# Expert loop of a two-block transformer kernel: activations 512 wide, bias products in four row groups, indices made ahead of the scatter, a new order over the chunks

## The chip, the cores and the metric

One core of one Trainium2 chip runs the whole program. The metric is the device time of one execution in microseconds; the time before is the median of 3 runs. The chip has a matrix engine (TensorE, PE in the profile, with PEld for its weight loads), a vector engine (DVE), a scalar engine (ACT), GpSimd (POOL) and SyncE (SP), which only issues transfers here. Each engine works off its own instructions in order; semaphores join them.

## The reference, cut to what matters

The program computes two blocks of a transformer over 512 tokens of width 1024. Only one part of the first block changes, the mixture of 32 experts of which each token takes 4:

```python
hg, hl = jnp.split(xblk @ w_gu[e] + b_gu[e], 2, axis=-1)
hg = jnp.minimum(hg, SWIGLU_LIMIT)
hl = jnp.clip(hl, -SWIGLU_LIMIT, SWIGLU_LIMIT)
glu = hg * jax.nn.sigmoid(hg * SWIGLU_ALPHA)
return ((hl + 1.0) * glu) @ w_down[e] + b_down[e]
```

`w_gu[e]` is 1024 x 2048, `w_down[e]` is 1024 x 1024, all float32. The rows are weighted by the gate and added into the tokens' rows of the output.

## The kernel before, in words

`experts` runs over 32 experts. An expert takes up to 128 tokens (slots) and 12 chunks of weights of 1 MB (128 x 2048 float32): chunks 0 to 7 are gate and value columns, 8 to 11 the down projection. Every float32 product is made from three products of a faster type: ACT copies a chunk from `raw` to its rounded part `wh` (`high_part`, line 2110), DVE subtracts to get the rest `wl` (`low_part`, line 2156), and PE multiplies for each of four k tiles `wh` with the high part of x, `wl` with it, and `wh` with the low part (lines 2080 to 2082): 12 matmuls of 512 columns a chunk. `raw` holds 6 chunks (SP reloads a place as soon as its `wl` is made, line 1994), `wh` and `wl` hold 4 (`PARTS`), so ACT may begin chunk m when PE has ended chunk m-4 (`used`).

The gate and value columns are cut in four groups g of 256+256 columns; a group takes two chunks (first and second half of k) and one bank of `pu`, two banks in turn. PE first puts the bias in with one product of 128 rows, of which only two rows of `brow` are not zero (line 2068). After chunks 3, 5, 7 and 9, ACT and DVE make `hb`, 256 wide, from group 0, 1, 2, 3 (`activate`), and PE turns it to `pt` by two transposes after chunks 3, 5, 7 and 8 (`turn`, line 2053); ACT and DVE split that to `hh` and `hl` (`turned_high`, line 2126, `turned_low`, line 2168) after chunks 5, 7, 9 and 10. Chunks 8 to 11 multiply these into `pd`.

Around this runs the traffic of tokens. DVE makes a selection matrix for the next expert (`select`, chunk 1), PE counts with it (`slots`, after chunk 2), DVE makes the indices (`index`, chunk 4, lines 2184 to 2188), POOL gathers the rows of x by them (line 2006), PE transposes these after chunks 8 and 9 (`turn_x`, line 2045, into `px`), ACT and DVE split them to `Xh` and `Xl` (lines 2130 and 2173) after chunks 10 and 11. The result goes back so: ACT multiplies `pd` with the gates to `y` (`weighted`, line 2116) at chunks 0 and 1 of the next expert, POOL adds the rows into memory by an indirect transfer (line 2018), waits for its landing (`scattered`), and counts up `returned`. `index` waits for `returned` (line 2184), since it overwrites `idx` and `gneg`, of which there are two places. The order on each engine is written out by hand; on POOL it is gather, bias, scatter, wait for the scatter's landing.

Of the kernel before, what the change touches and what calls it, by code (L numbers as in the profile page):

```python
# [6 lines left out]
F32 = mybir.dt.float32  # L7
I32 = mybir.dt.int32
# [1932 lines left out]
def experts(K, x, gate_rows, b_down, pos, gpart, w, bias, x_rows, y_rows, raw, loaded):  # L1941

    nc = K.nc
    with ExitStack() as ctx:
# [6 lines left out]
        brow = K.sb(ctx, "brow", [P, 2 * FE], F32R)  # L1951
# [3 lines left out]
        idx = K.sb(ctx, "idx", [P, 2], I32)  # L1955
        gneg = K.sb(ctx, "gneg", [P, 2])
        rl = K.sb(ctx, "rl", [P, 256])
        sg = K.sb(ctx, "sg", [P, 256])
        vc = K.sb(ctx, "vc", [P, 256])
        hb = K.sb(ctx, "hb", [P, 2, 256])  # L1960
# [4 lines left out]
        pu = K.ps(ctx, "pu", [P, 2, 512])  # L1965
        pd = K.ps(ctx, "pd", [P, 2, 512])
        px = K.ps(ctx, "px", [P, 2, 512])
        pt = K.ps(ctx, "pt", [P, 256])
        pslot = K.ps(ctx, "pslot", [P, 512])
        with stage(nc, "bias_in", "w_high", "w_low", "used", "relu", "sigmoid",  # L1970
                   "h_ready", "own", "turned", "t_high", "t_low", "sel_ready", "slots_ready", "idx_ready", "gathered",
                   "x_turned", "x_high", "x_low", "y_ready", "scattered", "trash_ready", "ones_ready", "spared", "issued", "returned", "down_made",
                   "down_added") as (block, *sems):
            (bias_in, w_high, w_low, used, relu, sigmoid, h_ready, own, turned, t_high, t_low, sel_ready, slots_ready,
             idx_ready, gathered, x_turned, x_high, x_low, y_ready, scattered, trash_ready, ones_ready, spared, issued, returned, down_made, down_added) = sems
# [23 lines left out]
            def _(pool):  # L1999
                def bias_of(e):  # L2000
                    pool.dma_start(brow[0:2, :].bitcast(F32), bias[bass.ds(e, 1), :, :].rearrange("a b n -> (a b) n")).then_inc(bias_in, 16)
# [7 lines left out]
                def expert(e, odd, first, last):  # L2009
                    if not last:  # L2010
# [3 lines left out]
                        pool.wait_ge(used, e * CHUNKS + 8)  # L2014
# [3 lines left out]
                    pool.indirect_dma_start(y_rows, bass.IndirectOffsetOnAxis(idx[:, odd:odd + 1], 0), y[:, odd, :], None,  # L2018
# [13 lines left out]
            def _(pe):  # L2032
# [1938 lines left out]
```

## Time and profile before

| | |
|---|---|
| median of 3 runs | 3823.16 us (3814.76 to 3829.57) |
| profiled execution | 3835.94 us, of it 3834.2 us span |
| PE, DVE, ACT busy over the span | 91%, 66%, 50% |
| expert loop | 632.5 to 1855 us of the span, 1222.5 us |
| PE, DVE, ACT busy in the loop | 1177.19, 1114.57, 941.03 us |
| granted TensorE clock, DMA share, rate in the loop | 1.00, 0.93, 338 GB/s |

A stretch of the busy table gives, for each engine, busy microseconds and instructions in brackets. Matmuls are pipelined: a matmul of 512 columns is shown as 0.39 us, yet the next starts about 0.23 us after it, so on PE starts are to be compared with starts. A bracket at a row's end is the idle time before it and the engine and line that ended it.

### The profile page before, as it was taken

The numbers are of one execution on the slowest core, as the hardware profiler recorded it, in microseconds if no ns is written. First come the engines' busy times: TensorE is split into PE (matmuls) and PEld (weight loads), VectorE is DVE, ScalarE is ACT, GpSimd is POOL, SyncE is SP. The second block draws the span as 40 slices with busy tenths as digits, with TensorE's granted clock in tenths as the row PEclk, the third lists the DMA queues.
The fourth block names the chain that finished last, engine by engine and source line by source line (L and its number), as shares of the span: only waits on it lengthen the run. The fifth ranks groups of instructions, "written<-read, shape, count | busy, mean of one in ns | idle before, by whom it ended". The sixth has DMA issues, their size and how long they took to land. (4 is left out here: it accounts for less than half of the span.)

```text
span 3834.2 us, 45928 instructions
## 1 busy us (share of the span) xinstructions
PE 3497.8 (91%) x16744; PEld 2766.1 (72%) x16744; DVE 2549.7 (66%) x3090; ACT 1934.5 (50%) x2320; POOL 216.6 (6%) x137
## 2 busy tenths in 40 slices
PE   9998776999999999999589898899998998799998
PEld 7875265777777777777458776678886876568886
DVE  6644545999999899999456757456625776646542
ACT  4213223777777777777345435444415435534422
POOL 0000000111111111111010000010001000000000
PEclk9987786999999999999899999899999999899999
DMA  4100025999999999999312111122322112023231
GB/s 145 45 23 23 0 109 206 342 348 343 345 341 346 345 352 346 345 351 346 118 47 77 50 61 55 46 86 95 104 83 72 56 50 82 17 62 108 96 105 61
DMA packets 113041, 597.08 MB, mean 156 GB/s; under 512 B 17554, under 2 KB 18850, under 8 KB 62562
## 3 DMA queue, kind: packets, MB, share of 16 engines
q1 hardware_dynamic: 102658, 577.78, 42.1%
q0 software_dynamic: 10240, 17.33, 1.8%
q8 instruction: 97, 1.59, 0.2%
q14 instruction: 46, 0.38, 0.0%
HBM read 585.01 MB, written 26.80 MB: 160 GB/s over the span
## 5 line engine op out<-in xcount | busy, mean ns | idle before, releaser
L2156 DVE TENSOR_TENSOR wl<-raw,wh 128x2048 fp32r<-128x2048 f32 x384 | 870.6, 2288 | 55.8 <-ACT wh L2110 55.6
L2110 ACT ACTIVATE wh<-raw 128x2048 fp32r<-128x2048 f32 x384 | 718.5, 1904 | 0.0
L2080 PE MATMUL pu<-wh,Xh 128*128 128x512 f32 x1024 | 405.7, 396 | 10.9 <-DVE wl L2156 10.9
L2082 PE MATMUL pu<-wh,Xl 128*128 128x512 f32 x1024 | 400.7, 391 | 0.0
L2081 PE MATMUL pu<-wl,Xh 128*128 128x512 f32 x1024 | 400.6, 391 | 0.0
L3815 ACT ACTIVATE w_high<-w_raw 128x1024 fp32r<-128x1024 f32 (+1 forms) x120 | 137.1, 1146 | 333.1 <-PE acc L3789 172.0
L3846 DVE TENSOR_TENSOR w_low<-w_raw,w_high 128x1024 fp32r<-128x1024 f32 (+1 forms) x120 | 159.6, 1331 | 195.0 <-PE ps L3747 103.5
L3771 PE MATMUL ps<-x_high,w_high 128*128 128x512 f32 x656 | 255.2, 389 | 0.0
L3772 PE MATMUL ps<-x_low,w_high 128*128 128x512 f32 x656 | 255.2, 389 | 0.0
L2080 PEld LDWEIGHTS pu<-wh,Xh 128*128 128x128 f32 x1024 | 193.0, 188 | 55.1 <-DVE wl L2156 17.5
L2730 PE MATMUL acc<-x_high,w_high 128*128 128x512 f32 x528 | 226.4, 429 | 0.0
L2082 PEld LDWEIGHTS pu<-wh,Xl 128*128 128x128 f32 x1024 | 192.6, 188 | 42.6
L2081 PEld LDWEIGHTS pu<-wl,Xh 128*128 128x128 f32 x1024 | 192.8, 188 | 40.3
L2731 PE MATMUL acc<-x_low,w_high 128*128 128x512 f32 x528 | 212.5, 402 | 0.0
L3332 DVE TENSOR_TENSOR w_low<-w_raw,w_high 128x1024 fp32r<-128x1024 f32 (+1 forms) x120 | 137.4, 1151 | 112.6 <-PE acc L2736 74.4
L2080 PE MATMUL pd<-wh,hh 128*128 128x512 f32 x512 | 210.8, 412 | 0.0
L2081 PE MATMUL pd<-wl,hh 128*128 128x512 f32 x512 | 202.3, 395 | 0.0
L2082 PE MATMUL pd<-wh,hl 128*128 128x512 f32 x512 | 201.4, 393 | 0.0
L3747 PE MATMUL ps<-x_high,w_low 128*128 128x512 f32 x704 | 173.2, 389 | 0.0
L3060 ACT ACTIVATE w_high<-w_raw 128x1024 fp32r<-128x1024 f32 (+1 forms) x120 | 119.2, 996 | 95.0 <-PE lev L2926 79.7
L3747 PEld LDWEIGHTS ps<-x_high,w_low 128*128 128x128 f32 x704 | 132.2, 188 | 27.5
L3784 PE MATMUL acc<-h_high,w_high 128*128 128x512 f32 x352 | 143.1, 407 | 1.5 <-DVE h_low L3880 1.5
(681 smaller groups left out, 7059.2 us busy)
## 6 DMA issues: line engine op xcount, KB each, us to landing
raw<-in_exp_w SPq DMA_DIRECT2D x384, 1024.0 KB, 7.1
w_raw<-in_w_in SPq DMA_DIRECT2D x100, 512.0 KB, 3.4
w_raw<-in_w_up SPq DMA_DIRECT2D x88, 512.0 KB, 3.7
w_raw<-in_w_down SPq DMA_DIRECT2D x32, 704.0 KB, 4.0
w_raw<-in_w_out SPq DMA_DIRECT2D x32, 384.0 KB, 3.1
w_raw<-in_w_mem_kv SPq DMA_DIRECT2D x16, 512.0 KB, 4.5
w_raw<-in_w_out SPq DMA_DIRECT2D x8, 512.0 KB, 4.2
w_raw<-in_ple_gate_w SPq DMA_DIRECT2D x8, 512.0 KB, 3.8
```

What stands on the lines that cost most here:

```text
L2080: nc.tensor.matmul(o, lh[:, k, :], wh[:, m % PARTS, c], start=(m >= 8 and kh == 0 and kk == 0), stop=False)
L2081: nc.tensor.matmul(o, lh[:, k, :], wl[:, m % PARTS, c], start=False, stop=False)
L2082: mm = nc.tensor.matmul(o, ll[:, k, :], wh[:, m % PARTS, c], start=False, stop=end)
L2110: nc.scalar.activation(wh[:, m % PARTS, :], raw[:, m % RAW, :], ACT.Copy).then_inc(w_high, 1)
L2156: nc.vector.tensor_tensor(wl[:, m % PARTS, :], raw[:, m % RAW, :], wh[:, m % PARTS, :], ALU.subtract).then_inc(w_low, 1)
L2730: nc.tensor.matmul(o, wh[:, n % 3, c], hi[:, k, :], start=(k == 0), stop=False)
L2731: nc.tensor.matmul(o, wh[:, n % 3, c], lo[:, k, :], start=False, stop=False)
L3747: mm = nc.tensor.matmul(o, wl[:, u % 2, c], high[:, k, :], start=False, stop=(k == DT - 1))
L3771: nc.tensor.matmul(o, wh(u)[:, c], high[:, k, :], start=(k == 0), stop=False)
L3772: nc.tensor.matmul(o, wh(u)[:, c], low[:, k, :], start=False, stop=False)
L3784: nc.tensor.matmul(o, wh(u)[:, c], hh[:, f * PART + k, :], start=(f == 0 and k == 0), stop=False)
L3846: nc.vector.tensor_tensor(wl[:, u % 2, 0:width(u)], raw[:, u % 3, 0:width(u)], wh(u), ALU.subtract).then_inc(low_ready, 1)
```

## The change

- `pu` has four banks, one for each of: gate columns 0 to 511, value columns 0 to 511, gate 512 to 1023, value 512 to 1023. Each takes two chunks. `px` has no banks of its own now: it is the first two banks of `pu`.
- All four bias products are made at the expert's start (`biases`), each from 32 partitions of its own (`brow[32g:32g+32]`), after waits for the bias and for both halves of x. `brow` is loaded by four small transfers in place of one.
- The activation works twice an expert, 512 wide, cut in `gate` (ACT), `gated` and `valued` (DVE); the turn of `hb` is four transposes, within chunk 5 (after its second k tile) and within chunk 9 (after its first). `turned_high` and `turned_low` are 512 wide, at chunk 8 and at chunk 0 of the next expert; there stands the splitting of x too. `weighted` moves from chunks 0 and 1 to 2 and 3.
- `index` no longer waits for `returned` and moves to chunk 5; the gates' sum and a copy of the index for the scatter (`back`) are made by `pay` at chunk 8, which waits for `returned`. `select` moves to chunk 2.
- POOL's bias transfers wait for chunk 1's end rather than for chunk 7's. The weights' layout in memory follows the new grouping; `rest_of_experts` reads it so.

The diff, cut:

```diff
-                    pool.dma_start(brow[0:2, :].bitcast(F32), bias[bass.ds(e, 1), :, :].rearrange("a b n -> (a b) n")).then_inc(bias_in, 16)
+                    for g in range(4):
+                        pool.dma_start(brow[32 * g:32 * g + 2, :].bitcast(F32),
+                                       bias[bass.ds(e, 1), :, g * 512:(g + 1) * 512].rearrange("a b n -> (a b) n")).then_inc(bias_in, 16)
...
-                        pool.wait_ge(used, e * CHUNKS + 8)
+                        pool.wait_ge(used, e * CHUNKS + 2)
...
                 def turn(e, c, first):
-                    pe.wait_ge(h_ready, e * 4 + (c + 1))
+                    pe.wait_ge(h_ready, e * 2 + (c + 1))
                     if not (first and c == 0):
-                        pe.wait_ge(t_low, e * 4 + c)
-                    for i in (0, 1):
-                        mm = nc.tensor.transpose(pt[:, i * P:(i + 1) * P], hb[:, c % 2, i * P:(i + 1) * P], K.c("ident"))
+                        pe.wait_ge(t_low, e * 2 + c)
+                    for i in range(4):
+                        mm = nc.tensor.transpose(pt[:, i * P:(i + 1) * P], hb[:, c, i * P:(i + 1) * P], K.c("ident"))
                     mm.then_inc(turned, 1)
 
+                def biases(e):
+                    pe.wait_ge(bias_in, e * 64 + 64)
+                    pe.wait_ge(x_low, e * 2 + 2)
+                    for g in range(4):
+                        nc.tensor.matmul(pu[:, g, :], ones[32 * g:32 * g + 32, :], brow[32 * g:32 * g + 32, :], start=True, stop=False)
+
                 def expert(e, odd, first, last):
+                    biases(e)
                     for m in range(CHUNKS):
                         kh, g = halves(m)
                         pe.wait_ge(w_low, e * CHUNKS + (m + 1))
                         if m < 8:
-                            o, lh, ll = pu[:, g % 2, :], Xh, Xl
-                            if kh == 0:
-                                if g == 0:
-                                    pe.wait_ge(bias_in, e * 16 + 16)
-                                    pe.wait_ge(x_low, e * 2 + 1)
-                                if not (first and g < 2):
-                                    pe.wait_ge(h_ready, e * 4 + (g - 1))
-                                nc.tensor.matmul(o, ones[:, :], brow[:, g * 512:(g + 1) * 512], start=True, stop=False)
-                            elif g == 0:
-                                pe.wait_ge(x_low, e * 2 + 2)
+                            o, lh, ll = pu[:, g, :], Xh, Xl
                         else:
                             o, lh, ll = pd[:, g, :], hh, hl
-                            pe.wait_ge(t_low, e * 4 + (4 if kh else 2))
+                            pe.wait_ge(t_low, e * 2 + (kh + 1))
                             if kh == 0 and not first:
                                 pe.wait_ge(y_ready, e * 2 + (g - 1))
                         for kk in range(4):
@@ -2080,16 +2081,19 @@
                             nc.tensor.matmul(o, lh[:, k, :], wh[:, m % PARTS, c], start=(m >= 8 and kh == 0 and kk == 0), stop=False)
                             nc.tensor.matmul(o, lh[:, k, :], wl[:, m % PARTS, c], start=False, stop=False)
                             mm = nc.tensor.matmul(o, ll[:, k, :], wh[:, m % PARTS, c], start=False, stop=end)
-                        mm.then_inc(used, 1)
-                        if m in (3, 5, 7, 8):
-                            turn(e, 3 if m == 8 else (m - 3) // 2, first)
+                            if kk == 3:
+                                mm.then_inc(used, 1)
+                            if (m, kk) == (5, 1):
+                                turn(e, 0, first)
+                            if (m, kk) == (9, 0):
+                                turn(e, 1, first)
                         if not last:
                             if m == 2:
                                 slots(e + 1)
                             if m in (8, 9):
                                 turn_x(e + 1, m - 8)
...
                     act.wait_ge(used, e * CHUNKS + (11 + d))
                     if d == 0:
                         act.wait_ge(returned, e + 1)
+                        act.wait_ge(paid, e * 2 + 2)
                     nc.scalar.activation(y[:, odd, d * 512:(d + 1) * 512], pd[:, d, :], ACT.Copy, scale=gneg[:, odd:odd + 1]).then_inc(y_ready, 1)
 
-                def activate(e, g):
-                    act.wait_ge(used, e * CHUNKS + (2 * g + 2))
-                    nc.scalar.activation(rl[:, :], pu[:, g % 2, 0:256], ACT.Relu, scale=-1.0, bias=top[:, 0:1]).then_inc(relu, 1)
-                    act.wait_ge(relu, e * 4 + (g + 1))
+                def gate(e, c):
+                    act.wait_ge(used, e * CHUNKS + (4 * c + 2))
+                    nc.scalar.activation(rl[:, :], pu[:, 2 * c, :], ACT.Relu, scale=-1.0, bias=top[:, 0:1]).then_inc(relu, 1)
+                    act.wait_ge(relu, e * 2 + (c + 1))
                     nc.scalar.activation(sg[:, :], rl[:, :], ACT.Sigmoid, scale=-SWIGLU_ALPHA, bias=top[:, 1:2]).then_inc(sigmoid, 1)
 
                 def turned_high(e, c):
-                    act.wait_ge(turned, e * 4 + (c + 1))
-                    nc.scalar.activation(hh[:, 2 * c:2 * c + 2, :], pt[:, :].rearrange("p (a b) -> p a b", a=2), ACT.Copy).then_inc(t_high, 1)
+                    act.wait_ge(turned, e * 2 + (c + 1))
+                    nc.scalar.activation(hh[:, 4 * c:4 * c + 4, :], pt[:, :].rearrange("p (a b) -> p a b", a=4), ACT.Copy).then_inc(t_high, 1)
 
                 def x_part(e, half):
                     act.wait_ge(x_turned, e * 2 + (half + 1))
@@ -2133,19 +2138,23 @@
                 def expert(e, odd, first, last):
                     for m in range(CHUNKS):
                         high_part(e, m, first)
-                        if not first and m < AHEAD:
-                            weighted(e - 1, 1 - odd, m)
-                        if m in (5, 7, 9, 10):
-                            turned_high(e, 3 if m == 10 else (m - 5) // 2)
-                        if m in (3, 5, 7, 9):
-                            activate(e, (m - 3) // 2)
-                        if not last and m >= 10:
-                            x_part(e + 1, m - 10)
+                        if not first:
+                            if m == 0:
+                                turned_high(e - 1, 1)
+                                x_part(e, 0)
+                                x_part(e, 1)
+                            if m in (2, 3):
+                                weighted(e - 1, 1 - odd, m - 2)
+                        if m in (5, 9):
+                            gate(e, (m - 5) // 4)
+                        if m == 8:
+                            turned_high(e, 0)
...
-                def activate(e, g):
-                    dve.wait_ge(relu, e * 4 + (g + 1))
-                    nc.vector.tensor_scalar(vc[:, :], pu[:, g % 2, 256:512], SWIGLU_LIMIT, -SWIGLU_LIMIT, ALU.min, ALU.max).then_inc(own, 1)
-                    dve.wait_ge(sigmoid, e * 4 + (g + 1))
+                def gated(e, c):
+                    dve.wait_ge(sigmoid, e * 2 + (c + 1))
                     nc.vector.scalar_tensor_tensor(sg[:, :], rl[:, :], SWIGLU_LIMIT, sg[:, :], ALU.subtract, ALU.mult).then_inc(own, 1)
-                    dve.wait_ge(own, e * 8 + (2 * g + 2))
-                    nc.vector.scalar_tensor_tensor(hb[:, g % 2, :], vc[:, :], 1.0, sg[:, :], ALU.add, ALU.mult).then_inc(h_ready, 1)
+
+                def valued(e, c):
+                    dve.wait_ge(used, e * CHUNKS + (4 * c + 4))
+                    nc.vector.tensor_scalar(vc[:, :], pu[:, 2 * c + 1, :], SWIGLU_LIMIT, -SWIGLU_LIMIT, ALU.min, ALU.max).then_inc(own, 1)
+                    dve.wait_ge(own, e * 4 + (2 * c + 2))
+                    nc.vector.scalar_tensor_tensor(hb[:, c, :], vc[:, :], 1.0, sg[:, :], ALU.add, ALU.mult).then_inc(h_ready, 1)
...
                 def index(e, odd):
                     dve.wait_ge(slots_ready, e + 1)
+                    nc.vector.tensor_scalar(spare[:, :], pslot[:, 3:4], trash[:, 1:2], trash[:, 0:1], ALU.mult, ALU.add).then_inc(spared, 1)
+                    dve.wait_ge(spared, e + 1)
+                    nc.vector.tensor_tensor(idx[:, odd:odd + 1], spare[:, :], pslot[:, 2:3], ALU.add).then_inc(idx_ready, 1)
+
+                def pay(e, odd):
+
                     dve.wait_ge(returned, e + 1)
-                    nc.vector.tensor_scalar(spare[:, :], pslot[:, 3:4], trash[:, 1:2], trash[:, 0:1], ALU.mult, ALU.add).then_inc(spared, 1)
-                    nc.vector.tensor_reduce(gneg[:, odd:odd + 1], pslot[:, 0:2], AX.X, ALU.add, negate=True).then_inc(spared, 1)
-                    dve.wait_ge(spared, e * 2 + 2)
-                    nc.vector.tensor_tensor(idx[:, odd:odd + 1], spare[:, :], pslot[:, 2:3], ALU.add).then_inc(idx_ready, 1)
+                    nc.vector.tensor_reduce(gneg[:, odd:odd + 1], pslot[:, 0:2], AX.X, ALU.add, negate=True).then_inc(paid, 1)
+                    dve.wait_ge(idx_ready, e + 1)
+                    nc.vector.tensor_copy(back[:, odd:odd + 1], idx[:, odd:odd + 1]).then_inc(paid, 1)
 
                 def expert(e, odd, first, last):
                     for m in range(CHUNKS):
+                        if m == 0 and not first:
+                            turned_low(e - 1, 1)
                         low_part(e, m)
+                        if m == 0 and not first:
+                            x_part(e, 0)
+                            x_part(e, 1)
                         if not last:
-                            if m == 1:
+                            if m == 2:
                                 select(e + 1, False)
-                            if m == 4:
+                            if m == 5:
                                 index(e + 1, 1 - odd)
-                        if m in (3, 5, 7, 9):
-                            activate(e, (m - 3) // 2)
-                        if m in (5, 7, 9, 10):
-                            turned_low(e, 3 if m == 10 else (m - 5) // 2)
-                        if not last and m >= 10:
-                            x_part(e + 1, m - 10)
+                            if m == 8:
+                                pay(e + 1, 1 - odd)
+                        if m in (5, 9):
+                            gated(e, (m - 5) // 4)
+                        if m in (6, 10):
+                            valued(e, (m - 6) // 4)
+                        if m == 8:
+                            turned_low(e, 0)
```

## Rows read from the trace of the kernel before

**Rows 1.** The page's section 5: the two instructions that split a weight chunk.
```profile
L2156 DVE TENSOR_TENSOR wl<-raw,wh 128x2048 fp32r<-128x2048 f32 x384 | 870.6, 2288 | 55.8 <-ACT wh L2110 55.6
...
L2110 ACT ACTIVATE wh<-raw 128x2048 fp32r<-128x2048 f32 x384 | 718.5, 1904 | 0.0
```

**Rows 2.** Busy by stretch (PE, PEld, DVE, ACT, POOL, clock, DMA share, GB/s): two experts, 29.
```profile
1424.28:1461.27 36.99, 36.44 (x170) 29.69 (x169) 34.83 (x35) 29.43 (x29) 4.65 (x3) 1.00 0.98 353
...
1689.71:1726.77 37.06, 36.44 (x170) 29.65 (x169) 34.97 (x35) 29.37 (x29) 4.77 (x3) 1.00 0.98 362
...
701.34:1803.04 1101.70, 1066.59 (x4873) 859.64 (x4873) 1011.07 (x987) 852.62 (x813) 136.76 (x88) 1.00 0.95 346
```

**Rows 3.** Timeline of PE (start, duration, line): turns, x transposes, bias products, chunk edges.
```profile
1008.41 0.39 PE L2082 MATMUL pd<-wh,hl 128*128 128x512 f32 x1
...
1009.42 0.41 PE L2053 MATMUL pt<-const,hb 128*128 128x128 f32 x2 [0.62 <-DVE hl L2168]
...
1012.90 0.60 PE L2045 MATMUL px<-const,rows 128*128 128x128 f32 x4
...
1013.26 0.48 PE L2080 MATMUL pd<-wh,hh 128*128 128x512 f32 x1
...
1013.58 0.40 PE L2081 MATMUL pd<-wl,hh 128*128 128x512 f32 x1
...
1016.14 0.40 PE L2080 MATMUL pd<-wh,hh 128*128 128x512 f32 x1
...
1018.94 0.40 PE L2068 MATMUL pu<-brow,ones 128*128 128x512 f32 x1
...
1019.17 0.40 PE L2080 MATMUL pu<-wh,Xh 128*128 128x512 f32 x1
...
1021.93 0.39 PE L2080 MATMUL pu<-wh,Xh 128*128 128x512 f32 x1
...
1030.83 0.38 PE L2053 MATMUL pt<-const,hb 128*128 128x128 f32 x2
...
1030.96 0.48 PE L2068 MATMUL pu<-brow,ones 128*128 128x512 f32 x1
...
1031.28 0.40 PE L2080 MATMUL pu<-wh,Xh 128*128 128x512 f32 x1
```

**Rows 4.** Timeline of DVE: the first of the index instructions in one expert.
```profile
1032.43 0.28 DVE L2185 TENSOR_SCALAR spare<-pslot,trash 128x1 f32<-128x1 f32 x1 [2.43 <-POOLq L2021]
```

**Rows 5.** Waits, 700 to 1700 us (total us, times, longest).
```profile
DVE spare L2185 <- POOLq L2021: 33.5, 22, 2.9
...
PE pt L2053 <- DVE hl L2168: 16.2, 27, 0.6
```

**Rows 6.** Timeline of ACT: the second product of the gate with y in one expert.
```profile
1019.13 0.69 ACT L2116 ACTIVATE y<-pd,gneg 128x512 f32<-128x512 f32 x1 [0.30 <-PE pd L2082]
```

**Rows 7.** Timeline of POOL, then landing times of lines 2018 (scatter) and 2006 (gather).
```profile
1020.72 1.93 POOL L2018 DMA_INDIRECT y_rows<-y,idx  x1 [13.73 <-ACT y L2116]
...
1033.83 2.29 POOL L2006 DMA_INDIRECT rows<-x_rows,idx  x1 [11.18 <-DVE idx L2188]
...
DMA to landing us min/median/max: 6.3/10.1/12.1
...
DMA to landing us min/median/max: 5.8/9.0/10.8
```

**Rows 8.** Stretch with six chunks loading alone; then line 1994's landing times.
```profile
604.00:606.00 2.00, 0.00 (x0) 0.00 (x0) 0.00 (x0) 0.00 (x0) 0.00 (x0) 0.50 1.03 434
...
DMA to landing us min/median/max: 4.7/7.1/9.7
```

**Rows 9.** By tile pu, pt and px: duration ns min/median/max, first and last start.
```profile
L2097 PEld LDWEIGHTS pu<-gate_rows,b_down x8: 283/327/333, 616.1 to 624.8; 32*128 32x128 f32 x8
...
L2168 DVE TENSOR_TENSOR hl<-pt,hh x128: 416/418/421, 654.9 to 1844.5; 128x256 fp32r<-128x256 f32 x128
...
L2173 DVE TENSOR_TENSOR Xl<-px,Xh x64: 679/683/692, 631.9 to 1811.5; 128x512 fp32r<-128x512 f32 x64
```

More of the change, by code:

```diff
@@ L1950, in experts @@
         sel = K.sb(ctx, "sel", [P, NT, SLOTS], F32R)
-        brow = K.sb(ctx, "brow", [P, 2 * FE], F32R)
+        brow = K.sb(ctx, "brow", [P, 512], F32R)
         ones = K.sb(ctx, "ones2", [P, P], F32R)
@@ L1955, in experts @@
         idx = K.sb(ctx, "idx", [P, 2], I32)
+        back = K.sb(ctx, "back", [P, 2], I32)
         gneg = K.sb(ctx, "gneg", [P, 2])
[L1957 to L1960, printed above, removed]
+        rl = K.sb(ctx, "rl", [P, 512])
+        sg = K.sb(ctx, "sg", [P, 512])
+        vc = K.sb(ctx, "vc", [P, 512])
+        hb = K.sb(ctx, "hb", [P, 2, 512])
         top = K.sb(ctx, "top7", [P, 2])
@@ L1964, in experts @@
         y = K.sb(ctx, "y", [P, 2, D])
[L1965 removed]
+        pu = K.ps(ctx, "pu", [P, 4, 512])
         pd = K.ps(ctx, "pd", [P, 2, 512])
[L1967 to L1968 removed]
+        pt = K.ps(ctx, "pt", [P, 512])
         pslot = K.ps(ctx, "pslot", [P, 512])
+        px = pu
         with stage(nc, "bias_in", "w_high", "w_low", "used", "relu", "sigmoid",
                    "h_ready", "own", "turned", "t_high", "t_low", "sel_ready", "slots_ready", "idx_ready", "gathered",
[L1972 to L1973 removed]
+                   "x_turned", "x_high", "x_low", "y_ready", "scattered", "trash_ready", "ones_ready", "spared", "issued", "returned", "paid",
+                   "down_made", "down_added") as (block, *sems):
             (bias_in, w_high, w_low, used, relu, sigmoid, h_ready, own, turned, t_high, t_low, sel_ready, slots_ready,
[L1975 removed]
+             idx_ready, gathered, x_turned, x_high, x_low, y_ready, scattered, trash_ready, ones_ready, spared, issued, returned, paid, down_made, down_added) = sems
             def halves(m):
@@ L2090, in expert @@
                                 turn_x(e + 1, m - 8)
-                down = [pu[:, 0, :], pu[:, 1, :], pd[:, 0, :], pd[:, 1, :]]
+                down = [pu[:, 2, :], pu[:, 3, :], pd[:, 0, :], pd[:, 1, :]]
                 slots(0)
@@ L2210, in _ @@
                 index(0, 0)
+                pay(0, 0)
                 nc.vector.memset(top[:, 0:1], SWIGLU_LIMIT).then_inc(ones_ready, 1)
@@ L2213, in _ @@
                 nc.vector.tensor_copy(ones[:, :], K.c("ones")).then_inc(ones_ready, 1)
-                for part in range(0, 2 * FE, P):
+                for part in range(0, 512, P):
                     ins = nc.vector.tensor_scalar(brow[:, part:part + P], K.c("ones"), 0.0, None, ALU.mult)
                 ins.then_inc(ones_ready, 1)
-                down = [pu[:, 0, :], pu[:, 1, :], pd[:, 0, :], pd[:, 1, :]]
+                down = [pu[:, 2, :], pu[:, 3, :], pd[:, 0, :], pd[:, 1, :]]
                 for i in range(DT):
@@ L2267, in _ @@
                             pe.wait_ge(glu, e * FJ + (j + 1))
-                            for bank, half in ((pg, 0), (pv, 256)):
-                                o = half + j % 2 * P
-                                b = j // 2 * 512 + o
+                            for bank, of in ((pg, 0), (pv, 1)):
+                                group, o = j // 4 * 2 + of, j % 4 * P
+                                b = group * 512 + o
                                 nc.tensor.matmul(bank[:, j % 2, :], brow[0:1, b:b + P], one_row[:, :], start=True, stop=False)
@@ L3904, in pack_experts @@
 def pack_experts(gu, down):
-    up = gu.reshape(EXPERTS, 2, 4, P, 2, 4, 256).transpose(0, 5, 1, 3, 2, 4, 6)
+    up = gu.reshape(EXPERTS, 2, 4, P, 2, 2, 512).transpose(0, 5, 4, 1, 3, 2, 6)
     dn = down.reshape(EXPERTS, 2, 4, P, 2, 512).transpose(0, 1, 4, 3, 2, 5)
@@ L3924, in lay_out @@
         "exp_w": pack_experts(i["exp_w_gu"][0], i["exp_w_down"][0]),
[L3926 removed]
+        "exp_b_gu": np.ascontiguousarray(i["exp_b_gu"][0].reshape(EXPERTS, 2, 2, 512).transpose(0, 2, 1, 3)).reshape(EXPERTS, 2 * FE),
         "exp_b_down": i["exp_b_down"][0],
```

13 lines of the change are left out of this document (7 added, 6 removed).

## The prediction

> **What bounds the kernel now.** I read the page's slices first: only the expert loop runs at a full clock with all engines and the DMA above nine tenths, and only the loop is changed. Then the busy table by expert: 29 experts take 1101.70 us, 37.99 each, while the fastest take 36.99 and 37.06 [rows 2]. Per expert PE is busy 1066.59/29 = 36.78 us, DVE 1011.07/29 = 34.86, ACT 852.62/29 = 29.40, so DVE has 3.1 us of air and PE almost none; PE is the engine to follow, and DVE feeds it. The granted clock is 1.00 there (2.4 GHz), so no gain lies in it.
>
> The waits then say what lies above 36.99. DVE waits 33.5 us in 1000 us for POOL's `returned` in front of `index`, up to 2.9 us at a time [rows 5]; in one expert it stood 2.43 us, until 11.71 us after the scatter had begun [rows 4, 7]. Behind it stood the next chunks' `wl`, and PE ran dry. Scatters land after 6.3 to 12.1 us [rows 7], which is why experts alternate between 37 and 39 us. The mean price is 37.99 - 36.99 = 1.00 us an expert. The fast experts keep one more stall: the last turn of `hb` and its wait for `hl`. The last matmul of chunk 8 starts at 1008.41, the next instruction could start 0.23 later, at 1008.64, and the transposes start at 1009.42 [rows 3]: 0.78 us, in each of 27 experts (the wait recurs with at most 0.6 us of modelled idle time [rows 5]). So PE's own work is 36.99 - 0.78 = 36.21 us an expert.
>
> **Part 1: index without the wait, `pay` late.** The wait goes to chunk 8 on DVE. Where is PE then? I count from the first bias product, T0. An up chunk is 1021.93 - 1019.17 = 2.76 at the head and about 2.73 on the mean of 12 matmuls at 0.2275 (my value, from 0.225 to 0.232 between starts), a down chunk 1018.94 - 1016.14 = 2.80 [rows 3]. DVE reaches `pay` after `wl` of chunk 8, which it can make once ACT has chunk 8 rounded, which needs PE's chunk 4 ended (T0 + 14.6); behind the activation that is about T0 + 19.2. The scatter begins 0.90 us after the second `y` is complete (1019.13 + 0.69 = 1019.82, scatter 1020.72 [rows 6, 7]). `weighted` now stands at chunks 2 and 3, where ACT gets to it at about T0 + 2.0 instead of T0 + 0.2, so the scatter begins at T0 + 3.6 instead of 1020.72 - 1018.94 = 1.8, and lands at the latest at T0 + 15.7. `pay` has 3.5 us of cover, so DVE's stall goes wholly: -1.00 us an expert. Its extra copy is a one-column instruction (0.15 to 0.28 us, [rows 4] for the longer one), on DVE's air. If the cover were gone, `pay` would cost PE nothing until PE had also used the 3 to 4 us that `wl` is ahead of it (below).
>
> What is late next: POOL. It still waits for the scatter's landing before the gather, in its own queue. Gather start = T0 + 3.6 + scatter + 0.9 (1033.83 - 1032.43, less 0.5 for the index instructions [rows 4, 7]); with the medians 10.1 and 9.0 [rows 7] the rows of x are there at T0 + 23.6. PE wants them after chunk 8: 0.45 (bias) + 8 x 2.73 + 0.45 (slots) + 0.45 (turn) + 2.80 = T0 + 26.0. Before, the same sum was 0.92 + 8 x 2.73 + 0.45 + 3 x 0.22 (turns, part 3) + 2.80 + 0.78 + 0.25 = T0 + 27.7, and up to 2.4 more where `index` stalled. Cover falls to 2.4 us; at the slowest of both, 12.1 + 10.8, it is late by 27.4 - 26.0 = 1.4. The spread of the two is about 1.3 us, so this happens now and then: I take 0.1 us an expert, with 0 and 1.4 as bounds. The four bias transfers come behind the gather on POOL and are covered by 12 us.
>
> **Part 2: bias products in row groups.** Before: four products, one in 1019.17 - 1018.94 = 0.23 us [rows 3], 0.92 us an expert. After: four of 32 rows one after another in the program. At best they run together: 0.23 us, gain 0.69. At worst they take turns as before: gain 0. Below nothing too: weights of 32 rows took 0.283 to 0.333 us to load [rows 9] at the half clock of that stage [rows 8], and I see no sign that few rows load sooner; four loads have to be made where one was, at 0.09 us or more each (a load and a transpose in 0.36/4 [rows 3]), and the load behind them needs the whole array. That could lose 0.2 us. I take 0.45 us for the block (four loads, then one product), a gain of 0.47. The Trainium skill (TensorE: Matmul & The Clock Gate, Part 3: Packing small matmuls) says that matmuls on four row groups ran 3.07 times as fast as one by one; 0.92/3.07 = 0.30 us would be its price, a gain of 0.62. No row here shows row groups.
>
> **Part 3: 512-wide activation.** PE: two transposes cost 0.13 + 0.32 - 0.23 = 0.22 us (1030.83, 1030.96, 1031.28), four cost 0.36 + 0.32 - 0.23 = 0.45 (1012.90, 1013.26, 1013.58) [rows 3]; four times 0.22 against twice 0.45 is even. DVE: 16 instructions of 0.418 us become 8 of 0.683 [rows 9]: 6.69 against 5.46, -1.2 us. ACT is likewise shorter. Nothing of that is on PE's path; DVE's air of 3.1 us becomes 2.0 in a shorter expert (35.8 - 34.86 + 1.23 - 0.15).
>
> **Part 4: the new order.** I walked one expert with a `wl` of 2.29 us (2.2 between starts) and a `wh` of 1.90 (1.8) [rows 1], each `wh` held back until PE has ended the chunk four earlier. `wl` is complete 3 to 4.5 us before PE wants it in every chunk. The first half's `hb` is complete at T0 + 14.9, its turn is due at 15.9. The second half's: DVE ends `wl` 10 at 25.3, then 1.35 us in `valued`, 26.65; the turn is due at 26.0 + 0.45 + 0.7 = 27.1, cover 0.45. Its low part is complete at 29.5, chunk 10 begins at 30.1, cover 0.6. x is split at T0 + 32.9, the bias products wait for it at 35.7. So the 0.78 us stall goes too: -0.78. The two thin covers are real: if either fails by 0.3 us it is paid once an expert.
>
> **Sum.** 36.21 - 0.47 + 0.1 = 35.84 us an expert, say 35.8, against 37.99: 2.2 us, by 30 experts 66, and 1 to 2 us for the first and last, which had no `returned` stall: 68. The fewer `brow` instructions at the start hide under PE's down products. Profiled execution 3835.9 - 68 = 3768. It stood 12.8 us above the median of 3823.2; from that, 3755.
>
> **The rivals.**
> A, the row groups take turns: 0.92 us, the rest as forecast; 36.3 an expert, 1.7 x 31 = 53, 3770. Nothing in the trace speaks against it.
> B, the DMA becomes the bound. It carries 353 GB/s x 36.99 us = 13.06 MB an expert, with a busy share of 0.98 [rows 2]; if busy means full, it ends at 360 GB/s and an expert at 36.3, and with bursts uneven 36.5: 1.5 x 31 = 46, 3777. Against it: with chunks alone the same engines moved 434 GB/s at 1.03 [rows 8], ACT never waited for a chunk (the idle time before `wh` is 0.0) [rows 1], and chunks landed in 4.7 to 9.7 us [rows 8] where the ring leaves 13. The Trainium skill (DMA: Bandwidth & Descriptors, Where 436 GB/s comes from) says that loads from HBM are bound at about 358 GB/s a core, by which an expert takes 13.06/358 = 36.5 us, rival B's time; the 434 GB/s of this trace, also from HBM, speaks against that rule here.
> C, the gather is late as a habit, by 1 us on the mean, because at a higher rate both indirect transfers land about 1.7 us later each: 36.8, 1.2 x 31 = 37, 3786.
> D, slower than before: the same chain, scatter's landing, POOL, gather, `turn_x`. It decides when scatter plus gather exceed 26.0 - 4.5 + 2.15 = 23.7 us on the mean, against 19.1 by medians and 22.9 by the two slowest. With the slowest of both and one chunk more (1 MB at 434 GB/s, 2.4 us) in front, 25.3, PE stands 3.8 us at `turn_x`: 39.5 an expert, +1.5 x 31 = 47, 3870.
>
> **How the numbers follow.** Forecast 0.52; A 0.15; B 0.13; C 0.10; D 0.05; something between C and D that ends near the old time 0.05. The forecast's own range is 3738 to 3770: the bias block from 0.23 to 0.7, the gather from 0 to 0.4, and 7 us for medians of a few runs. To hold 8 in 10 the range must reach over A, B and most of C: 3734 to 3796. About 0.5% (19 us) is what a measurement here can tell from no change. Faster by more: forecast, A, B and nearly all of C, 0.88; within: 0.07; slower: 0.05.
>
> **What would show each step.** After: no DVE wait at `index`, and none to speak of at `pay`; an expert every 35.8 us; in PE's timeline 0.3 to 0.5 us from the first bias product to the first weight product (0.9 if A); no wait of the transposes in chunk 9 for `hb`, or that margin was wrong; the x transposes waiting for the gather only in a few experts (C, D if in most); ACT waiting for a DMA if B. The prediction is wrong if PE's own work isn't 35.7 us, which its matmul starts would show, or if the landing times of the indirect transfers grow by over 2 us each.

## The result, and the profile after

The changed kernel takes 3763.97 us (median of 4 runs, 3754.99 to 3776.01) against 3825.81 for the kernel before on the same occasions: a ratio of 0.9837, 95% interval 0.9815 to 0.9858, 62 us faster. 3755 was forecast, with a range of 3734 to 3796. Later, in a comparison of its own, it took 3762.07 us, a ratio of 0.9826 (0.9808 to 0.9845).

Most of the gain lies in the expert loop. Between the two profiled executions the span fell by 59.8 us, where 68 was forecast: 52.3 of it from the loop's first bias product to its last down product, about 7 behind the loop. That last stretch took 1973.6 to 1982.9 us in the fourteen profiled executions of this document, longest in the kernel before, so most of those 7 us may be variation from run to run; whether the change has a share in them is open. The first two experts became 2.3 us slower together (76.75 to 79.03), where the forecast had a small gain; one part of that is a late gather, the rest was not traced.

The lines of the page after that answer to those of before (the splits of a chunk are those of [rows 1]):

```profile
span 3774.4 us, 45043 instructions
PE 3472.6 (92%) x16744; PEld 2751.5 (73%) x16744; DVE 2520.7 (67%) x2854; ACT 1906.4 (51%) x2128; POOL 271.2 (7%) x233
...
L2165 DVE TENSOR_TENSOR wl<-raw,wh 128x2048 fp32r<-128x2048 f32 x384 | 873.5, 2286 | 58.7 <-ACT wh L2114 58.5
L2114 ACT ACTIVATE wh<-raw 128x2048 fp32r<-128x2048 f32 x384 | 735.4, 1916 | 191.2 <-PE pu L2083 144.5
```

ACT now stands 191.2 us before its `wh`, because PE has not yet freed a place, where it stood 0.0 before: the feeding engines are ahead of PE nearly all the time. The busy table by expert, with the columns of [rows 2]; three experts, then 29 of them:

```profile
900.64:940.45 39.81, 37.63 (x169) 30.34 (x168) 34.32 (x28) 28.59 (x23) 7.62 (x6) 0.96 0.92 337
940.45:976.23 35.78, 35.78 (x169) 29.16 (x168) 33.99 (x28) 28.49 (x23) 5.51 (x6) 1.00 0.99 359
...
1515.24:1551.02 35.78, 35.78 (x169) 29.16 (x168) 33.93 (x28) 28.49 (x23) 6.11 (x6) 1.00 1.00 377
...
718.72:1766.61 1047.89, 1041.57 (x4873) 845.88 (x4872) 986.47 (x783) 826.79 (x638) 187.66 (x174) 1.00 0.98 363
```

An undisturbed expert takes 35.78 us, PE busy in all of it; the mean is 1047.89/29 = 36.13 us, against 37.99. The difference of 0.35 us is in a few experts, and the waits of that stretch (total us, times, longest) say where:

```profile
PEld pu L2048 <- DMA rows<-x_rows,idx: 11.4, 14, 2.7
PEld pu L2063 <- issue: 10.4, 29, 0.4
PE pu L2048 <- DMA rows<-x_rows,idx: 6.2, 4, 2.3
```

Line 2048 is the transpose of x: it waits for the gather. PE stands idle for it in 4 of the 29 experts, and in 14 its weight load comes later for it. There is no wait of DVE for `returned` any more and none of PE for `hb` or `hl`, where [rows 5] had 33.5 and 16.2 us. The landing times (min/median/max) of the scatter, then the gather, and both on POOL's timeline:

```profile
DMA to landing us min/median/max: 6.3/11.3/12.6
...
DMA to landing us min/median/max: 4.6/9.7/11.7
...
1012.01 2.40 POOL L2021 DMA_INDIRECT y_rows<-y,back  x1 [19.10 <-ACT y L2121]
1024.95 1.65 POOL L2009 DMA_INDIRECT rows<-x_rows,idx  x1 [10.54 <-issue]
```

The expert begins at 1008.46 here. The scatter starts 3.55 us into it, as walked (3.6), and the gather 16.5 us into it, where the walk with the medians of before had 14.6.

### The profile page after: what moved, and what is told of

Read it like the earlier page. It is cut to its first block and busy times, and to the rows that moved or that the text cites. A ratio compares the mean times of both kernels' runs of the same rounds, so it can differ in the third digit from the quotient of the medians.

```text
span 3774.4 us, 45043 instructions
## 1 busy us (share of the span) xinstructions
PE 3472.6 (92%) x16744; PEld 2751.5 (73%) x16744; DVE 2520.7 (67%) x2854; ACT 1906.4 (51%) x2128; POOL 271.2 (7%) x233
## 5 line engine op out<-in xcount | busy, mean ns | idle before, releaser
L2114 ACT ACTIVATE wh<-raw 128x2048 fp32r<-128x2048 f32 x384 | 735.4, 1916 | 191.2 <-PE pu L2083 144.5
```

Of the source, the lines that this page charges most:

```text
L2114: nc.scalar.activation(wh[:, m % PARTS, :], raw[:, m % RAW, :], ACT.Copy).then_inc(w_high, 1)
```

## The experiments

Two theories stood at the start. Mine: PE's own work bounds the loop, and the gain is the sum of stalls and instructions taken out of PE's line, with a rest lost to late gathers. The rival: something the change brings besides (512-wide instructions, fewer instructions on DVE and ACT, another rhythm of the loads) is what pays. The first four kernels take parts one at a time; the others test what is left. Totals of variants that differ by a few us have overlapping intervals; there the time from one expert's first bias product to the next one's, read from the traces, decides. In undisturbed experts of one kernel it repeats within 0.1 us or better.

**Indices without the wait, alone, in the kernel before.**

```diff
                 def index(e, odd):
                     dve.wait_ge(slots_ready, e + 1)
-                    dve.wait_ge(returned, e + 1)
...
+                            if m == 8:
+                                pay(e + 1, 1 - odd)
```

> The kernel before, with one part of the change: the indices are made without waiting for the scatter's return, and the gates' sum and a copy of the index for the scatter are made at chunk 8, behind that wait. My theory: the stall of DVE at the index goes, every expert takes the 37.0 us of the fast ones instead of 38.0, the gain is 1.0 x 30 = 30 us (3795 against 3825). Rival: the wait only moves, to POOL, which starts the gather after the scatter has landed, and PE then waits at the transposes of x: 38 us an expert, no gain. By the medians the rows of x are there at 1.8 + 10.1 + 0.9 + 9.0 = 21.8 us after the expert's first bias product, and PE wants them at 27, so I expect no such wait.

Measured: 3797.25 us against 3829.64, ratio 0.9912 (0.9896 to 0.9929), 32 us. Every expert after the first takes 36.95 to 37.00 us; the alternation is gone. What is left in its waits is the old stall at the last turn:

```profile
PEld pt L2054 <- DVE hb L2166: 31.7, 29, 1.1
PE pt L2054 <- DVE hl L2170: 20.1, 29, 0.7
```

The wait was worth 1.02 us an expert and did not move to POOL: there the scatter starts early in the expert and the gather has room.

**The last turn inside chunk 9, alone and with the first.**

```diff
-                        if m in (3, 5, 7, 8):
-                            turn(e, 3 if m == 8 else (m - 3) // 2, first)
...
+                            if (m, kk) == (9, 0):
+                                turn(e, 3, first)
```

> The kernel before, with one thing changed: the last turn of hb stands in chunk 9 behind its first k tile instead of after chunk 8. My theory: the 0.78 us stall that every expert of the kernel before has at that turn goes, 0.7 to 0.8 x 32 = 22 to 25 us (3801), and the stalls behind the index stay. Rival: the stall moves to chunk 10, which needs the low part of the same turn, ready no earlier than about 1.9 us after chunk 9's start and behind a wl on DVE; then the gain is 0.3 us an expert or less, under 10 us.

> The kernel before with both parts: index free of the scatter's return, last turn inside chunk 9. If the two stalls are separate, 1.0 + 0.78 us an expert, about 55 us, 3770, and all that the changed kernel has beyond that is its bias block (0.4 to 0.5 us an expert, 15 us) less its late gathers (0.35 us, 11 us). Rival: the stalls overlap, or DVE (34.9 us of work in an expert of 36.2) becomes the bound: 36.7 or more, 3785 or above.

Measured: alone 3813.83 us, ratio 0.9957 (0.994 to 0.9974), 16 us, between the theory's 22 to 25 and the rival's 10; both 3783.14, ratio 0.988 (0.9864 to 0.9897), 46 us, 36.46 us an expert. The two add up (32 + 16), but the turn is worth 0.51 us an expert (36.97 - 36.46), not 0.78. The stall itself went wholly (0.86 us in the kernel with the index alone, none here). The waits of the kernel with both show part of what was given back:

```profile
PEld pu L2069 <- issue: 11.6, 28, 0.5
PEld pd L2081 <- DVE wl L2161: 6.9, 29, 0.2
```

The last turn had shared one break in the weight products with the transposes of x; alone it needs a break of its own (a place where other instructions stand between weight products). With the distances between PE's starts added up by kind over 28 experts of each kernel, the price of 0.35 us is: 0.09 for the late start behind the new break, 0.12 in the weight products, where PE now meets `wl`, 0.10 behind the bias products, and 0.15 in front of the first of them, less 0.11 in the transposes. The 0.15 is a wait for something that the profile does not name ("issue"): the first bias product starts 0.33 and 0.44 us after the product before it, in turn from expert to expert. In the kernel with the index alone that distance is 0.23.

**Bias products one after another, with 128 rows, in the changed kernel.**

```diff
-                        nc.tensor.matmul(pu[:, g, :], ones[32 * g:32 * g + 32, :], brow[32 * g:32 * g + 32, :], start=True, stop=False)
+                        nc.tensor.matmul(pu[:, g, :], ones[:, :], brow[:, g * 512:(g + 1) * 512], start=True, stop=False)
```

> The changed kernel with its four bias products of 128 rows each, one after another, as the kernel before makes them, at the expert's start; brow is 2048 wide and loaded by one transfer again. My theory: the row groups work, the block grows from about 0.55 us to about 0.95, fastest experts 36.15 instead of 35.78, 10 to 15 us slower than the changed kernel (3776). Rival A: row groups bring nothing and the time is that of the changed kernel (35.8). Rival B: the four small transfers on POOL make the gather late, so with one transfer the late gathers go and the median is no worse.

Measured: 3772.65 us, ratio 0.9848 (0.9831 to 0.9864); the fastest experts take 35.98 us (36.15 was expected), 0.20 more than 35.78. The mean is 36.21, with late gathers as in the changed kernel (landings of 11.4 and 9.8 us), so the four small transfers are not their cause. PE's timeline, first the changed kernel, then this one:

```profile
1008.13 0.40 PE L2083 MATMUL pd<-wh,hl 128*128 128x512 f32 x1
1008.46 0.51 PE L2063 MATMUL pu<-brow,ones 32*128 32x512 f32 x4
1008.90 0.50 PE L2081 MATMUL pu<-wh,Xh 128*128 128x512 f32 x1
1009.24 0.40 PE L2082 MATMUL pu<-wl,Xh 128*128 128x512 f32 x1
```

```profile
1035.06 0.40 PE L2081 MATMUL pd<-wh,hl 128*128 128x512 f32 x1
1035.30 1.08 PE L2061 MATMUL pu<-brow,ones 128*128 128x512 f32 x4
```

In row groups the four products start within 0.01 us of each other and take 0.44 us to the next start, but the first starts 0.33 - 0.23 = 0.10 late and the product behind them costs 0.34 - 0.23 = 0.11 more: 0.65 us. With 128 rows the block runs on without a gap, 0.92. That makes 0.27, and the periods give 0.20: the weight products outside the block take 0.06 us more in the kernel with row groups (the first ones behind it start every 0.235 to 0.24 us). The weight loads of both kernels at the same place:

```profile
1008.46 0.19 PEld L2063 LDWEIGHTS pu<-brow,ones 32*128 32x128 f32 x4 [0.36 <-issue]
1008.90 0.19 PEld L2081 LDWEIGHTS pu<-wh,Xh 128*128 128x128 f32 x1 [0.25 <-issue]
```

```profile
1035.06 0.89 PEld L2061 LDWEIGHTS pu<-brow,ones 128*128 128x128 f32 x4
```

With 128 rows each load starts with the product before its own, 0.23 us ahead. At the change from 128 to 32 rows, and at the change back, it starts only with its own product (1008.46 and 1008.90).

**The same with 32 rows in one row group** (on the changed kernel with `y` earlier, below).

```diff
+                        nc.tensor.matmul(pu[:, g, :], ones[0:32, :], brow[0:32, g * 512:(g + 1) * 512], start=True, stop=False)
```

> The same kernel, with the four bias products of 32 rows all on the first 32 partitions (brow 2048 wide again, one transfer). With 128 rows each one after another the block took 0.92 us, in four row groups 0.44 with 0.2 around it, and the expert 0.20 less. If the gain is that of four groups at once, one group takes the 0.92 us again, 36.0 an expert. If it is that of fewer rows, 35.8 stays.

Measured: 3783.75 us in a single run; 36.45 us an expert, 0.67 more than in four groups, and 0.47 more than with 128 rows.

```profile
1039.03 1.21 PE L2061 MATMUL pu<-brow,ones 32*128 32x512 f32 x4
1040.17 0.51 PE L2079 MATMUL pu<-wh,Xh 128*128 128x512 f32 x1
```

Both readings that I had written were off: one group takes not 0.92 but 1.14 us, with the same late starts around it. Four groups do run together (1.14 becomes 0.44), but 32-row products among 128-row ones cost more than 128-row ones do. The dearer part is at the edges: the second, third and fourth start 0.24 us apart, as full ones nearly do, while from the first to the second it is 0.34, and from the last to the weight product 0.32. That fits the loads above, which are not hidden where the row count changes; why they are not is not shown.

**The gather ahead of the wait for the scatter; `y` a chunk earlier.** Two independent cures of late gathers.

```diff
                         gather(e + 1, 1 - odd)
+                    if not first:
+                        pool.wait_ge(scattered, e * 16)
+                        pool.sem_inc(returned, 1)
```

```diff
-                            if m in (2, 3):
-                                weighted(e - 1, 1 - odd, m - 2)
+                            if m in (1, 2):
+                                weighted(e - 1, 1 - odd, m - 1)
```

> The changed kernel, where POOL starts the next gather as soon as its indices are made, and waits for the last scatter's landing only behind it. My theory: the late x transposes (the mean expert of 36.13 us against 35.78 for the undisturbed) come from POOL's queue, which holds the gather back until the scatter has landed; now the gather starts at about 11.6 us of an expert instead of 15, lands 3 us earlier, no expert waits for it, all take 35.8, 0.35 x 31 = 11 us less than the changed kernel. Rival: gather and scatter in flight together slow each other, landing times of both grow by 3 us or more, and the transposes of x wait as before (no gain).

> The changed kernel with the gate products of y behind chunks 1 and 2 on ACT instead of 2 and 3. My theory: the scatter starts 1.8 us earlier, so does the gather, and of the waits of up to 2.3 us at the x transposes only a rest of under 0.05 us an expert stays: 35.8 us, about 10 us less than the changed kernel. Rival: ACT waits for the last chunk's end before the second product, high parts come later, and PE waits for wl: 36.2 or more.

Measured: 3756.13 us (ratio 0.9821, 0.9805 to 0.9837) and 3759.08 us (0.9824, 0.9807 to 0.984). In both all experts after the first take 35.7 to 35.8 us and no wait for the gather is left. POOL with the gather first:

```profile
1030.29 2.40 POOL L2025 DMA_INDIRECT y_rows<-y,back  x1 [20.68 <-ACT y L2126]
1038.52 2.84 POOL L2009 DMA_INDIRECT rows<-x_rows,idx  x1 [5.83 <-DVE idx L2202]
```

It starts 8.2 us after the scatter instead of 12.9. So the late gathers come from POOL's queue. The rival was half right: landing in company takes longer (gather 10.4 us at the median instead of 9.7), which eats 0.7 of the 4.7 us. With `y` earlier, the scatter lands after 10.1 us at the median and the gather after 8.9, at a rate of 367 GB/s, where the changed kernel had 11.3 and 9.7 at 363: the load's mean rate alone does not set them. Nor does the moment of the start alone: the kernels below that also have `y` earlier and the old order on POOL land the gather after 8.5 to 8.7, but the scatter after 10.7 to 11.6. What sets the scatter's time is open.

**The wait put back into the changed kernel.**

```diff
                 def index(e, odd):
                     dve.wait_ge(slots_ready, e + 1)
+                    dve.wait_ge(returned, e + 1)
```

> The changed kernel with the one wait put back: the index waits for the scatter's return again. Two readings of what the wait costs. If its cost is the 1.0 us an expert of the kernel before, 37.1 us an expert and about 3795. If my walk through the new order holds, DVE reaches the index 10.3 us into the expert and the scatter returns at 15.1, a stall of 4 to 5 us; the first half of hb is then ready at 19 to 20 while PE wants to turn it at 15.9, so PE stands 3 to 4 us in every expert: 39 to 40 us, 3860 to 3890, slower than the kernel before. If the lead of wl over PE (3 to 4 us) absorbed it: 36.2, 3765.

Measured: 3863.84 us, ratio 1.0107 (1.0084 to 1.0129): slower than the kernel before. An expert takes 39.35 us.

```profile
DVE spare L2196 <- POOLq L2024: 99.3, 29, 5.4
PEld pt L2056 <- DVE hb L2175: 88.3, 44, 4.8
PE pt L2056 <- DVE hb L2175: 68.3, 28, 4.4
```

DVE stands 99.3/29 = 3.4 us an expert, PE at the first turn up to 4.4. One wait that cost 1.0 us in the old order costs 39.35 - 36.13 = 3.2 in the new one: the two parts of the change need each other. Some 0.6 of the 3.2 is not the wait itself but the lower of TensorE's two clock levels, which follows many of these stalls (last section); the granted clock of the 29 experts is 0.98 on the mean.

**The 512 width by itself** (on the kernel with `y` earlier): each 512-wide instruction of the activation and of the split of `hb` is cut in two.

```diff
-                    nc.vector.tensor_scalar(vc[:, :], pu[:, 2 * c + 1, :], SWIGLU_LIMIT, -SWIGLU_LIMIT, ALU.min, ALU.max).then_inc(own, 1)
+                    for h in (slice(0, 256), slice(256, 512)):
+                        ins = nc.vector.tensor_scalar(vc[:, h], pu[:, 2 * c + 1, h], SWIGLU_LIMIT, -SWIGLU_LIMIT, ALU.min, ALU.max)
+                    ins.then_inc(own, 1)
```

> The kernel with the gate products of y behind chunks 1 and 2 (no late gathers, every expert 35.78 us), with each 512-wide instruction of the activation and of the split of the turned hb cut in two of 256, on ACT and DVE. The 512 width by itself. My theory: PE is the bound and DVE has 1.8 us of air an expert; DVE gets 8 x (2 x 0.418 - 0.683) = 1.2 us more, that leaves 0.6, and the one thin cover, hb before the second turn (0.3 to 0.4 us), shrinks by 0.15: an expert stays at 35.8 to 35.9, under 5 us in all. Rival: DVE at 35.2 of 35.8 us can't keep its lead any more, PE waits for hb or wl, 36.3 or more, 15 us.

Measured: 3766.68 us, ratio 0.9832 (0.9815 to 0.9849), 35.94 us an expert instead of 35.78. DVE is busy 1005.10 of 1042.32 us and keeps its lead; what gives is the one thin cover, in every expert:

```profile
713.05:1755.37 1042.32, 1042.32 (x4873) 844.01 (x4872) 1005.10 (x1016) 849.45 (x813) 160.15 (x175) 1.00 0.98 366
...
PEld pt L2056 <- DVE hb L2186: 10.8, 29, 0.4
```

So in the new order the width is worth 0.16 us an expert (35.94 against the 35.78 of the kernel with `y` earlier), through `hb` before the second turn, which starts 0.10 us late on the mean, and not through DVE's total.

**Fewer breaks, and the best of all.** On the kernel with `y` earlier, the count of slots goes to the bias products and its selection on DVE to chunk 0; then the gather first as well.

```diff
                 def expert(e, odd, first, last):
+                    if not last:
+                        slots(e + 1)
                     biases(e)
```

> The same kernel, with the count of slots (four small matmuls) moved from behind chunk 2 to the expert's start, right in front of the bias products, and its selection on DVE from chunk 2 to chunk 0. Each break in the row of weight products costs 0.09 to 0.1 us beside its own instructions, because the first product behind it starts late. My theory: two breaks become one, 35.68 us an expert instead of 35.78, 3 us in all. Rival: the selection on DVE in front of the second chunk of the expert makes wl late or the slots wait for it, and the expert takes 35.8 or more.

> The changed kernel with all that helped: gate products of y behind chunks 1 and 2, the count of slots at the expert's start, and the gather started before the wait for the last scatter's landing. No expert waits for the gather: 35.6 us an expert in all of them, 0.5 us less than the changed kernel's mean of 36.13, 16 us in all, 3748. Rival: scatter and gather in flight together slow the weights' chunks, ACT waits for a chunk, and the time is that of the slots variant with the old order on POOL (3756) or worse.

> The changed kernel as it is, on the same chip as the combined version, so that the two can be compared: 3764, and between 0 and 4 us of waits at the x transposes per ten experts, since these come from the landing times of scatter and gather, which vary.

Measured: slots first 3756.53 us, ratio 0.9816 (0.9796 to 0.9837), 35.64 us an expert instead of 35.78; with the gather first too 3753.77 us (3748 was expected), ratio 0.9807 (0.9788 to 0.9827), with 35.6 us in every one of 29 experts (1033.37 us in all); the changed kernel beside it 3762.07, with 35.99 us an expert on the mean and one of 38.7. The combined version is ahead of the changed kernel by 8 us between medians; their intervals overlap, so for the total that is an indication, while the periods are clear. Two breaks made one, in PE's timeline:

```profile
1033.03 0.50 PE L2039 MATMUL pslot<-gpart,sel 128*128 x4
1033.45 0.51 PE L2063 MATMUL pu<-brow,ones 32*128 32x512 f32 x4
1033.89 0.50 PE L2083 MATMUL pu<-wh,Xh 128*128 128x512 f32 x1
```

## Why the prediction was right, and where its steps were not

Per expert, in the order in which the runs took the parts:

| step | forecast | measured | from |
|---|---|---|---|
| index without the wait | -1.00 | -1.02 | 37.99 to 36.97, index alone |
| last turn's stall | -0.78 | -0.51 | 36.97 to 36.46, with the turn |
| four banks, two wide turns, new order | 0 | -0.48 | 36.46 to 35.98, serial bias, fastest experts |
| bias products in row groups | -0.47 | -0.20 | 35.98 to 35.78, fastest experts |
| late gathers | +0.1 | +0.35 | 35.78 to 36.13, mean |
| sum | -2.15 | -1.86 | 37.99 to 36.13 |

**Bound.** PE's own work was put at 35.74 us and measured at 35.78. That is partly luck: of its terms two were too large by 0.27 each, and one that stood at nothing was 0.48. The total was lucky too: the first two experts lost 2.3 us where a gain was forecast, and the kernel's end gave about 7 us that no step of the prediction had.

**Index.** Right in mechanism and size, also that `pay` would be covered: DVE has no wait there. What hid it is the time between the scatter's return and chunk 8: in the expert shown above `pay` ran 19.3 us into it, as walked (19.2), and the gather, which stands behind the return on POOL, had begun 2.8 us earlier.

**Last turn.** The mechanism was right, the term too large. "The 0.78 us stall goes too" left out that the turn had shared its break with the transposes of x and that the shift meets other small waits: 0.86 us of stall went, 0.35 came back elsewhere.

**Row groups.** The block was put at 0.45 us and takes 0.65. The step that failed is "four loads, then one product": 0.44 us between starts is near it, but I had counted no late start in front and behind, though the rows of x transposes showed one of 0.09 behind each break [rows 3]. The figure of the Trainium skill (TensorE: Matmul & The Clock Gate, Part 3: Packing small matmuls), 3.07 times as fast as one by one, would have given 0.92/3.07 = 0.30 us, an estimate. Against 32-row products in one group, the four groups here are 1.14/0.44 = 2.6 times as fast; against the 128-row products that they replace, with what stands around them, only 0.92/0.65 = 1.4 times.

**New order and width.** Forecast as even on PE, and the step that failed is that it counted only the transposes. Between the kernel with both parts and that with serial bias the sums of PE's starts give: 0.15 us less in front of the first bias product (0.38 on the mean against 0.24), 0.27 less in the bias products, which no longer stand behind breaks, 0.19 less in the weight products, where PE no longer meets `wl`, and 0.17 more in the transposes; a few hundredths are spread over the rest. The width's 0.16 is not one of these: it shows as a wait for `hb`, and the kernel with both parts, 256 wide, has no such wait. In the new order the width keeps that wait away. Whether DVE's shorter work or the new order took away the wait for `wl` was not separated.

**Late gathers.** The mechanism is the one named as next to be late, the place is POOL's queue, and the term was a third of what it should have been. The step that failed is the use of the medians 10.1 and 9.0 of before. In the new order they are 11.3 and 9.7, 1.9 us more together, and a cover of 2.4 us becomes 0.5. The size varies: in the second profiled execution of the changed kernel the same term is 35.99 - 35.78 = 0.21.

**The rivals.** A (row groups take turns) fell with the 0.44 us. B (DMA the bound) fell too: ACT waited for PE and never for a chunk, and the loop moved 363 GB/s on the mean, up to 377 in one expert and 410 in 10 us (1535 to 1545 us). The Trainium skill's rule of about 358 GB/s a core from HBM (DMA: Bandwidth & Descriptors, Where 436 GB/s comes from) does not hold for such stretches. The loop's mean tests it little: the 363 include the scatter, and the weight chunks alone, 12 of 1.05 MB in 35.78 us, make 352. C is what happened, at a third of its size or less. Its reason is shown in part: from 346 over 355 and 360 to 363 GB/s (the kernel before, index alone, both, changed) the scatter's median grows from 10.1 over 10.5 and 11.0 to 11.3 us, but with `y` earlier it is 10.1 at 367. D did not happen: it needed landings of 23.7 us together, and the medians make 21.0.

## What to carry to other kernels

Where PE is the bound, count the breaks in its row of products and the waits that end on it, part by part, and treat a stall on a timeline as an upper bound: 0.51 us of 0.78 was gained. Moving a stall's cause also moves what stands behind it, so add up all distances between starts, not the one stall. A wait that is moved off one engine still stands in the queue of another (here POOL), and latencies of transfers measured in the old schedule are not those of the new one; here they grew by 1.9 us together. Small products in row groups paid much against small products in one group, and little against full ones that run without a gap.

## What was not expected of the hardware

A PE stall of 2.2 us can cost 1.5 us on top of itself. In two experts the transposes of x waited about equally long for the gather; the changed kernel's PE timeline, of the first one and of the second:

```profile
812.88 0.39 PE L2083 MATMUL pd<-wh,hl 128*128 128x512 f32 x1
815.54 0.66 PE L2048 MATMUL pu<-const,rows 128*128 128x128 f32 x4 [2.27 <-DMA rows<-x_rows,idx]
...
817.40 0.39 PE L2082 MATMUL pd<-wl,hh 128*128 128x512 f32 x1
817.63 0.40 PE L2083 MATMUL pd<-wh,hl 128*128 128x512 f32 x1
```

```profile
922.96 0.39 PE L2083 MATMUL pd<-wh,hl 128*128 128x512 f32 x1
925.53 0.66 PE L2048 MATMUL pu<-const,rows 128*128 128x128 f32 x4 [2.18 <-DMA rows<-x_rows,idx]
...
928.52 0.63 PE L2083 MATMUL pd<-wh,hl 128*128 128x512 f32 x1
928.94 0.63 PE L2081 MATMUL pd<-wh,hh 128*128 128x512 f32 x1
```

After the first the products start every 0.23 us again; about 1 us after the second they start every 0.43 us for some 3 us, the lower of the two clock levels (1.2 GHz), and the expert takes 39.81 us instead of 38.30 (granted clock 0.96 in the table of experts above). In the kernel with serial bias a stall of 1.92 us did the same: a granted clock of 0.64 in the 4.7 us behind it.

The kernel with the wait put back has such stalls in nearly every expert. Two of its first turns, and a product a little later:

```profile
1597.51 0.66 PE L2056 MATMUL pt<-const,hb 128*128 128x128 f32 x4 [2.80 <-DVE hb L2175]
...
1599.39 0.39 PE L2081 MATMUL pu<-wh,Xh 128*128 128x512 f32 x1
```

```profile
1635.92 0.66 PE L2056 MATMUL pt<-const,hb 128*128 128x128 f32 x4 [2.08 <-DVE hb L2175]
...
1637.84 0.63 PE L2082 MATMUL pu<-wl,Xh 128*128 128x512 f32 x1
```

The stall of 2.80 us is not followed by the lower level, the one of 2.08 is. Of the 27 first turns there whose start is 1.6 us or more behind the product before, 13 are followed by it, for some 3 us and three times for some 7; over 29 experts that costs 18 us, 0.6 an expert. In the second execution of the changed kernel a stall of 2.67 us stayed without it (an expert of 38.7 us). So the length of the stall alone does not decide; what does is open.
